# Modulation weights of 80 of 96 tiles, streamed through the prompt attention of a hybrid decoder step

## What is computed

```python
def adaln(c, w, b):
    m = jax.nn.silu(c) @ w + b
    return jnp.split(m, 6, axis=-1)
...
def modulate(x, g, shift, scale):
    return rms_norm(x, g) * (1 + scale[:, None, :]) + shift[:, None, :]
...
    for i in range(DEPTH):
        sh_mp, sc_mp, g_mp, sh_fp, sc_fp, g_fp = adaln(c_prompt, ada_w[i], ada_b[i])
        sh_ms, sc_ms, g_ms, sh_fs, sc_fs, g_fs = adaln(c_sample, ada_w[i], ada_b[i])
        hp = modulate(xp, norm_mix_pre[i], sh_mp, sc_mp)
...
            op = mla_out(mla_prompt_attend(ql, qr, ckv, kr), mla_w_uv[j], mla_w_o[j])
...
        xp = xp + g_mp[:, None, :] * rms_norm(op, norm_mix_post[i])
        hp = modulate(xp, norm_ffn_pre[i], sh_fp, sc_fp)
```

## Time and profile before

| | |
|---|---|
| median of 3 runs | 2793.55 us (2793.35 to 2793.69) |
| the profiled execution's own time | 2793.25 us |
| its span | 2791.4 us |
| PE busy | 2554.5 us, 92% of the span |
| DVE busy | 1784.6 us, 64% |
| ACT busy | 1347.5 us, 48% |
| mean granted TensorE clock | 0.967 of 2.4 GHz |
| mean DMA traffic | 91 GB/s |

### The profile page before, as it was taken

One profiled execution on the slowest core, in us unless ns is written; L12 is line 12 of the kernel. 1 busy time (PEld: TensorE's weight loads), 2 busy tenths in 40 slices (PEclk: granted clock), 3 DMA queues, 4 the chain that ended last, 5 costly groups with the idle time before them and its releaser, 6 DMA issues.

```text
span 2791.4 us, 49092 instructions
## 1 busy us (share of the span) xinstructions
PE 2554.5 (92%) x18538; PEld 2305.3 (83%) x18538; DVE 1784.6 (64%) x3297; ACT 1347.5 (48%) x2943; POOL 320.9 (11%) x349
## 2 busy tenths in 40 slices
PE   5969688999878888999999999999997999999996
PEld 2549466666655788999999999999997999999995
DVE  3972255555562335886666885877885687776666
ACT  4852234333441356554445655555553555544444
POOL 0000000000000052300002311301412320200003
PEclk9979899999998999999999999999999999999998
DMA  7931100000007331223232222224328222242221
GB/s 307 392 126 43 40 23 12 12 11 26 0 7 277 133 105 61 84 84 91 85 91 99 84 84 69 84 83 107 98 77 66 76 84 85 90 122 85 91 90 62
DMA packets 93278, 254.66 MB, mean 91 GB/s; under 512 B 36082, under 2 KB 40562, under 8 KB 89106
## 3 DMA queue, kind: packets, MB, share of 16 engines
q1 hardware_dynamic: 92354, 251.18, 29.1%
q10 hardware_dynamic: 720, 0.71, 0.1%
HBM read 244.79 MB, written 7.07 MB: 90 GB/s over the span
## 4 chain that ended last, share of the span: by engine, by line
PE 48%; DVE 10%; ACT 3%; issue 2%; POOL 1%; DMA 1%; POOLq 0%; ACTq 0%; DVEq 0%
PE psum L2385 10%; PE psum L2384 10%; PE psum L2383 10%; PE psum L2358 5%; PE psum L2360 5%; PE psum L2359 5%; DVE t_conv L2219 2%; DVE t_w_lo L2201 2%; DVE t_y L2251 1%; PE psum L2340 1%; PE psum L1922 1%; PE psum L2342 1%; PE psum L2341 1%; DMA t_raw<-in_ffn_w 1%; DVE t_scaled L1696 1%
## 5 line engine op out<-in xcount | busy, mean ns | idle before, releaser
L2383 PE MATMUL psum<-t_h,t_w_hi 128*128 128x272 f32 x2816 | 816.8, 290 | 3.2 <-DVE t_w_lo L2201 3.2
L2385 PE MATMUL psum<-t_h,t_w_lo 128*128 128x272 f32 x2816 | 812.8, 289 | 0.0
L2384 PE MATMUL psum<-t_h,t_w_hi 128*128 128x272 f32 x2816 | 811.7, 288 | 0.0
L2383 PEld LDWEIGHTS psum<-t_h,t_w_hi 128*128 128x128 f32 x2816 | 531.6, 189 | 4.6 <-DVE t_w_lo L2201 3.4
L2384 PEld LDWEIGHTS psum<-t_h,t_w_hi 128*128 128x128 f32 x2816 | 531.9, 189 | 1.2
L2385 PEld LDWEIGHTS psum<-t_h,t_w_lo 128*128 128x128 f32 x2816 | 531.4, 189 | 0.0
L2219 DVE SCALAR_TENSOR_TENSOR t_conv<-t_u,t_taps,t_conv 128x272 f32<-128x272 f32 (+2 forms) x528 | 340.0, 644 | 151.3 <-ACT t_conv L2123 145.1
L2358 PE MATMUL psum<-t_g_hi,t_w_hi 128*128 128x272 f32 x1408 | 410.2, 291 | 28.1 <-DVE t_w_lo L2201 16.5
L2251 DVE TENSOR_TENSOR t_y<-psum,t_y 128x272 f32<-128x272 f32 x640 | 279.9, 438 | 202.2 <-PE psum L2360 198.0
L2359 PE MATMUL psum<-t_g_lo,t_w_hi 128*128 128x272 f32 x1408 | 405.1, 288 | 0.0
L2360 PE MATMUL psum<-t_g_hi,t_w_lo 128*128 128x272 f32 x1408 | 404.4, 287 | 0.0
(11 more groups left out here) (201 smaller groups left out, 3886.4 us busy)
## 6 DMA issues: line engine op xcount, KB each, us to landing
t_raw<-in_ffn_w SPq DMA_DIRECT2D x264, 512.0 KB, 3.6
ada_w<-in_ada_w SPq DMA_DIRECT2D x24, 2048.0 KB, 10.7
cache<-in_cache SPq DMA_DIRECT2D x64, 320.0 KB, 5.0
t_raw<-in_wo SPq DMA_DIRECT2D x16, 512.0 KB, 3.7
pair_raw<-in_pair_w SPq DMA_DIRECT2D x8, 768.0 KB, 4.2
x<-in_x SPq DMA_DIRECT2D x1, 4352.0 KB, 22.5
x<-in_x SPq DMA_DIRECT2D x2, 2176.0 KB, 9.7
out_x_out<-x SPq DMA_DIRECT2D x4, 1088.0 KB, 6.5
```

The lines of the kernel that those rows point to most:

```text
L2383: pe.matmul(bank, t.w_hi[s][:, o], hi, start=kt == 0, stop=False)
L2384: pe.matmul(bank, t.w_hi[s][:, o], lo, start=False, stop=False)
L2385: last = pe.matmul(bank, t.w_lo[s][:, o], hi, start=False, stop=kt == KT - 1)
```

## The change

The modulation stage keeps 4 groups (`ADA_FIRST`), tiles 0 to 15. It is unrolled, has a buffer for each group, and x comes in three chunks, each issued in front of one of the first three groups. The norm of chunk m now stands around the split and the products of group m. One gain fold stays, the other seven go to the start of the sample stage, on DVE.

The other 80 tiles become 40 units of two tiles (1 MB each), five for each head pair, in steps 10 to 14. Their weights aren't split: the products are plain fp32, with the conditioning vectors padded to 32 columns as weights. The eight k tiles go to four groups of 32 output partitions, k tile 0 and 4 to the first, 1 and 5 to the second, and so on, so the sum over the four groups is left for the turn, whose right-hand side `k.fold` has four stacked identities. In a step n:

- PE: scores, then the turn of the unit of step n - 1, then the values (even n), then **the products of this step's unit**, and behind them the transposes.
- ACT: after the exponentials, the copy of the unit of step n - 1 (128x256).
- DVE: at the step's end, the sum with the bias of that unit.
- SP: unit u + 2 is loaded when the products of unit u are done, behind the pair weights of its pair.

The products and the turned result live in bank 7, one unit at a time: the products wait for `late_taken` of the unit before. The copy buffer of the projection stage for the samples' rows now lies in the memory of `wuk`, which isn't loaded yet then.

```diff
+ADA_FIRST = 2 * KT // ADA_GROUP
+LATE_W = 2 * P
+LATE_A_PAIR = 5
...
         def _(sp):
             sp.dma_start(c[:], io["cond"]).then_inc(small_in, 16)
+            for m in range(ADA_FIRST):
+                if m < NC:
+                    t0, n = CHUNKS[m]
+                    sp.dma_start(k.x[:, :, t0:t0 + n], io["x"][:, :, t0:t0 + n]).then_inc(x_in[m], 16)
+                sp.dma_start(w[:, m, :], io["ada_w"][m]).then_inc(w_in[m], 16)
...
+            for m in range(ADA_FIRST):
+                if m < NC:
+                    act.wait_ge(x_in[m], 16)
+                    x_norm.act_squares(k, act, m)
+                act.wait_ge(w_in[m], 16)
                 for h in range(2):
                     cols = slice(h * HALF, (h + 1) * HALF)
...
+                    act.activation(w_hi[:, m % 2, cols], w[:, m, cols], ACT.Copy).then_inc(hi_ready, 1)
+                if m < NC:
+                    x_norm.act_root(k, act, m)
+                if m:
+                    copy_rows(m - 1)
+            copy_rows(ADA_FIRST - 1)
...
+            def load_late(u):
+                if u >= 2:
+                    sp.wait_ge(late_done, u - 1)
+                sp.dma_start(late_w[u % 2][:], io["ada_late"][u]).then_inc(late_in[u % 2], 16)
...
+            for i in range(HP):
+                if i + 2 < HP:
+                    load(i + 2)
+                for h in range(LATE_A_PAIR):
+                    u = LATE_A_PAIR * i + h + 2
+                    if u < LATE_UNITS:
+                        load_late(u)
             sp.dma_start(m.wuk[:], io["wuk"]).then_inc(wuk_in, 16)
...
+            def copy_late(unit):
+                if unit:
+                    u, _, _ = unit
+                    act.wait_ge(late_done, u + 1)
+                    wait(act, late_turned, u)
+                    act.activation(late_rows[:], late_out, ACT.Copy).then_inc(late_copied, 1)
...
                     exp(n)
+                    copy_late(late(jj, b, n - 1))
...
+                    dve.wait_ge(late_turned, u + 1)
+                    dve.tensor_tensor(flat[:, tiles, :], late_turn.rearrange("p (m s) -> p m s", s=N_SEQ),
+                                      k.bias[:, tiles].unsqueeze(2).to_broadcast([P, 2, N_SEQ]), ALU.add)\
+                       .then_inc(late_taken, 1)
...
                     lo(n)
+                    take_late(late(jj, b, n - 1))
...
+            def late_products(jj, unit):
+                if unit:
+                    u, slot, turn = unit
+                    pe.wait_ge(late_in[slot], 16 * turn + 16)
+                    wait(pe, late_taken, u)
+                    for kt in range(KT):
+                        r = slice(32 * (kt % 4), 32 * (kt % 4) + 32)
+                        last = pe.matmul(late_out[r, :], k.cond[:, kt, :], late_w[slot][:, kt * LATE_W:(kt + 1) * LATE_W],
+                                         start=kt < 4, stop=kt >= 4)
+                    last.then_inc(late_done, 1)
+
+            def turn_late(unit):
+                if unit:
+                    u, _, _ = unit
+                    pe.wait_ge(late_copied, u + 1)
+                    for a in range(2):
+                        last = pe.matmul(late_turn[:, a * N_SEQ:(a + 1) * N_SEQ], late_rows[:, a * P:(a + 1) * P],
+                                         k.fold[:], start=True, stop=True)
+                    last.then_inc(late_turned, 1)
...
                 for n in range(STEPS):
                     if not (last and n + 2 >= STEPS):
                         score(*at(i, n, 2), s if n + 2 < STEPS else 1 - s)
                     if n in SLOT_OF_JOB and not last:
                         job(i + 1, SLOT_OF_JOB[n], 1 - s)
+                    turn_late(late(jj, b, n - 1))
                     if n % 2 == 0 and not (first and n == 0):
                         values(*at(i, n, -1), s if n else 1 - s)
...
+                    late_products(jj, late(jj, b, n))
                     turn(*at(i, n, 0))
...
             last.then_inc(rot_set, 1)
+            for n in range(1, 8):
+                fold_gain(k, dve, n // 4, n % 4).then_inc(folded, 1)
+            dve.wait_ge(folded, 7)
```

More of the change, by code:

```diff
@@ L220, in adaln_stage @@
         block = own.enter_context(nc.Block())
-        def run(step, eng, between=lambda: None):
-            for s in range(ADA_SLOTS):
-                step(s, s, True)
-            between()
-            def rest(n):
-                for s in range(ADA_SLOTS):
-                    step(n * ADA_SLOTS + s, s, False)
-            with eng.Fori(1, GROUPS // ADA_SLOTS) as n:
-                rest(n)
-        def wait(eng, sem, value, first):
-            if not first or value > 0:
-                eng.wait_ge(sem, value)
         @block.sync
@@ L274, in step @@
[L274 to L282 removed]
+                    if m >= 2:
+                        act.wait_ge(used, 2 * m + h - 3)
@@ L290, in turn @@
                 for a in range(ADA_GROUP):
[L291 to L292 removed]
+                    last = pe.matmul(k.banks[4 + m % 2][:, a * N_SEQ:(a + 1) * N_SEQ],
+                                     rows[:, m, a * P:(a + 1) * P], pair_fold[:], start=True, stop=True)
                 last.then_inc(turned, 1)
[L295 to L299 removed]
+            pe.wait_ge(parts, 2)
@@ L326, in _ @@
-            flat, flat_bias = k.ada[:].rearrange("p l m s -> p (l m) s"), bias[:].rearrange("p l m -> p (l m)")
-            def take(m, s, first):
-                wait(dve, turned, m + 1, first)
-                tiles = bass.ds(m * ADA_GROUP, ADA_GROUP)
+            dve.tensor_tensor(pair_fold[:], k.ident[0:2 * N_SEQ, 0:N_SEQ], k.ident[0:2 * N_SEQ, N_SEQ:2 * N_SEQ], ALU.add)\
+               .then_inc(folds, 1)
+            by_32 = [k.ident[:, 32 * q:32 * q + N_SEQ] for q in range(4)]
+            dve.tensor_tensor(k.fold[:], by_32[0], by_32[1], ALU.add).then_inc(folds, 1)
@@ L331, in take @@
+            for q in (2, 3):
+                dve.wait_ge(folds, q)
+                dve.tensor_tensor(k.fold[:], k.fold[:], by_32[q], ALU.add).then_inc(folds, 1)
+            flat = k.ada[:].rearrange("p l m s -> p (l m) s")
+            def take(m):
+                dve.wait_ge(turned, m + 1)
+                tiles = slice(m * ADA_GROUP, (m + 1) * ADA_GROUP)
                 dve.tensor_tensor(flat[:, tiles, :],
-                                  k.banks[4 + s % 2][:, 0:ADA_GROUP * N_SEQ].rearrange("p (m s) -> p m s", s=N_SEQ),
@@ L341, in step @@
                        .then_inc(lo_ready, 1)
-                if not (first and s < 2):
-                    take(m - 2, (s - 2) % ADA_SLOTS, first)
-                if first and s > X_JOBS:
-                    x_norm.dve(k, dve, s - X_JOBS - 1)
-            def x_rest():
-                for j in range(ADA_SLOTS - X_JOBS - 1, NC):
-                    x_norm.dve(k, dve, j)
-            run(step, dve, x_rest)
-            for m in (GROUPS - 2, GROUPS - 1):
-                take(m, m % ADA_SLOTS, False)
```

230 lines of the change are left out of this document (119 added, 111 removed).

## The result

The changed kernel took **2780.39 us** (median of 4 runs, 2779.33 to 2781.96), the kernel before on the same chip 2793.62 us: a ratio of 0.9945, interval 0.993 to 0.996. It is faster by 13.2 us; the forecast was 26.5 us, so half of it came. The profiled execution took 2779.85 us with a span of 2778.0.

A forecast was written before the change was run, and what follows sets the result against it. DMA was taken to bound the modulation stage and PE the attention, where DMA is free. 2793.25 - 113.8 (shorter stage) + 86.4 (units, 10.8 a pair over 8 pairs) + 1 = 2767 us; range of 8 in 10: 2750 to 2804.

The forecast's parts named there:

- The modulation stage: First stage, cut from 24 groups to 4: first projection matmul at 57 (range 54 to 62) instead of 170.8, -113.8 us.
- for group 3 no norm is in the way: split to 47.6, remainder to 50.4: Modulation stage, last group: after the remainder, products to 52.3 and gain fold to 54.8, then projection at 56.
- The side at the low clock: End of the modulation stage: the last half's products at the low clock would add 2 us.
- The products: Attention, PE: four parts side by side, 0.88 us a unit, with width changes 5.1 us a pair for five units.
- The turns: Attention, PE behind the next step's scores: two matmuls a unit, 0.48 us with the tail, 2.4 us a pair.
- The waits for ACT's copy: Attention, before the turns: PE idles 0.75, 0.5, 0.6, 2.15 and 1.4 us in steps 11 to 15, 5.4 a pair.
- The waits for the take: Steps 11 and 13: products wait until DVE took the turned result, 0.45 us each, 0.9 a pair.
- The cover that goes: Attention, steps 10 to 15: PE's earlier waits of 2.98 us a pair vanish because units fill them, counted as -3.0.
- The extra wait instructions and register steps on PE: Attention, PE: two or three more a step, may add 0.1 each; put at +1 us.
- The rest: Behind the attention: seven gain folds moved to the sample stage's start, 0 to 1.1 us, taken as 0; tail unchanged.
- the marks that were to show it: Projection at 57, records 0.055 apart, copy waits 5 us a pair, pairs of 71 to 72.5 us, no late-weight wait.
- if PE waits for anything else: Steps 10 to 15: any PE wait not forecast there, or a first stage ending after 65, makes the forecast wrong.

The follow-up runs named there:

- a_recip: Changed kernel with VectorE's reciprocal root of each token chunk behind the next group's remainder split, not in front: 2773.65 us, ratio 0.9935 to the kernel before.
- a_behind: Changed kernel with each unit's products behind the transposes of its step, not in front: 2745.39 us, ratio 0.9835 to the kernel before.
- a_best: Changed kernel with pair loop written out on all three engines, reciprocal roots behind the remainders and products behind the transposes: 2723.79 us, ratio 0.9751.
- a_two_parts: Changed kernel with each unit's eight products on two 32-column parts of the array instead of four: 2813.54 us, ratio 1.0084 to the kernel before.
- a_one_part: Changed kernel with all eight products of a unit on one 32-column part of the array: 2882.32 us in a single execution.
- a_units_out: Changed kernel without the 40 units (loads, products, copies, turns, takes), modulation preset to a constant: 2688.31 us, ratio 0.9633 to the kernel before.

## Why the prediction was right in direction and 13 us off

Direction and range were right (2780 in 2750 to 2804), the likeliest value 13 us too low. Step by step, against the changed kernel's trace:

- **The modulation stage**: 62.5 instead of 57, -108.3 instead of -113.8; just outside the range given for it (54 to 62). The step that failed is the one on group 3, "for group 3 no norm is in the way: split to 47.6, remainder to 50.4". The norm of chunk 2 was in the way on DVE, since its reciprocal is queued in front of the remainder. ACT's split ended at 50.1 and the remainder at 57.0. I walked ACT's and PE's queues and took DVE for free. Turning the two round (a_recip) brings the stage to 59.3, so this step is 3.2 of the 5.5 us; ACT's split was also 2.5 us later than walked, and that part was not followed up. The side at the low clock (2 us for the last half's products) was named and did not come in this run, but did in others.
- **The products**: 5.1 a pair, 41 in all. Measured 46.3 of busy time, and 42.8 in a_behind and a_best. Busy time holds the last record's modelled end; from a unit's first record to the transposes' first it is 1.00 us in 35 of the 40 units and 1.27 to 1.87 in the other five, 43.4 in all. The kind (four parts side by side) is shown by a_two_parts and a_one_part.
- **The turns**: 19.2 forecast, 24.7 measured (L1057 x160), 22.0 in a_behind.
- **The waits for ACT's copy**: 43.2 forecast, 32.9 measured. From the transposes' end to the turn I walked 2.35 to 2.46 us; it is 2.13 and 2.05 (444.58 to 446.71, 449.89 to 451.94). In steps 13, 14 and 15 the waits are 0.4, 1.8 and 1.2 instead of 0.6, 2.15 and 1.4.
- **The waits for the take**: 7.2 forecast, 8.4 measured, in 16 waits, as said in steps 11 and 13 only.
- **The cover that goes**: 24 forecast, 26 measured (35.4 in a_units_out, 9.4 left).
- These five: 86.4 forecast, 86.3 measured. That they agree is luck: products, turns and the take's waits were 12.2 higher, the copy's waits and the cover 12.3 the other way. The step that failed is what stands beside them: the stalls at the loop's jumps, 11.5 us, for which the sum had nothing. "The extra wait instructions and register steps on PE ... I put +1" looked at the time in which instructions are issued, and not at the fetch that a longer body brings at the jump, nor at the weights' transfers that stand in its way.
- The stretch grew by 92.1, not by 87.4. Counted from start to next start, which leaves the modelled ends out, products are 43.4 (forecast 40.8), turns with the take's waits 30.8 (26.4), the copy's waits 32.9 (43.2), the stalls 11.5 (1) and the cover 26 (24): 92.6. So the 4.7 us are what is left when the stalls, products and turns stand against copy waits that were walked 10 us too long.
- **The rest** of the kernel, behind the attention, is 2.8 us longer (1966.8 against 1964.0), forecast 0. In the other kernels with the change it is 1959 to 1966, so this is scatter and not the gain folds, as far as these runs can tell.

5.5 + 4.7 + 2.8 = 13.0 us are the whole difference between 2767 and 2780.

Of the marks that were to show it, these came: records side by side and 16 in 1.07 us (in groups of four, and not one by one 0.055 apart), the turn's waits largest in steps 14 and 15 (32.9 / 8 = 4.1 a pair, forecast 5), no wait for late weights (1024 KB in 4.9 us), 68.9 to 72.1 us from pair to pair (by DVE's L914) but for the two distances with a jump in them. The first projection matmul was late. The warning "if PE waits for anything else" was limited to steps 10 to 15; the stalls are behind step 15, in front of the first scores of the next pair.

## What to carry to other kernels

Work that is put into a hardware loop can cost instruction fetches besides time: compare the records of one turn of the loop before and after, look at whether the instruction queues' transfers stop within the loop and whether an engine stands idle by "issue" at the jump, and write the loop out where it does (14.9 us here, nothing in the kernel before). Transfers alone are no sign of a loss: a_units_out has them on q14 and no stall. A wait of one engine for a short step on another is shortened most cheaply by the order on the other one: one pair of lines turned round gave 30 us, more than twice what the whole change gave, and the cover that seemed to pay for the old order was there in either. When a stage is walked to find its end, all queues are walked; a short instruction that waits in front of a long one that doesn't was 3 us of this stage (62.5 against 59.3).

## What the hardware showed that I had not expected

- PE, whose loop body was fetched anew in every turn, stalled at each jump: 5.1 and 6.4 us with the weights' transfers under way, 2.3 us each without, 0 when written out. The clock falls there (0.72 over 12 us); 3.4 of the 14.9 us that the written-out loop gives are not the waits themselves.
- DVE stalls there for itself: with PE's loop written out, its stalls stayed (9.2 us in two), but without the weights' transfers it had none. q14, the queue that serves DVE, ACT or both, fetched at the jumps in a_units_out too, though their turns are as long as in the kernel before, where it was silent, and nothing stalled.
- 32-column fp32 products of 256 columns on four parts: 1.07 us for eight matmuls, 1.92 to 2.01 on two parts, 3.75 on one.
- Instruction transfers start late beside the weights': behind the first jump 3.7 and 4.1 us after the branch, 1.0 and 1.1 us with the loads left out.
